# Position-bias tables read back from DRAM in final orientation, instead of turned on TensorE

## The chip, the cores and the metric

One Trainium2 chip, one core of it. The metric is the device time of one execution in microseconds (us). Engines: PE is TensorE, DVE is VectorE, ACT is ScalarE, POOL is GpSimd, SP is SyncE, which here only issues DMAs. Everything is fp32; the big products are split into a high and a low part and done as three products.

## The reference, cut to what matters

Two blocks of two layers each over 256 tokens of width 1024. The change touches only the position bias of the two attentions of the second block:

```python
REL_BUCKETS, REL_MAX_EXACT, REL_MAX_DIST, ATTN_HEADS = 32, 16, 128, 8

def t5_bucket(dist):                 # dist = query_pos - key_pos
    n = jnp.maximum(dist, 0)
    nf = jnp.maximum(n, 1).astype(jnp.float32)
    large = 16 + (jnp.log(nf / 16) / math.log(8) * 16).astype(jnp.int32)
    return jnp.where(n < 16, n, jnp.minimum(large, 31))
```

The logit of query q and key k in head h gets `rel_bias[t5_bucket(q - k), h]` added before the softmax. Keys after the query are masked; the window attention ("even" layer) also masks keys 128 or more behind. So the bias of a head depends on q - k alone: 384 numbers for each of 8 heads and 2 attentions hold all of it, and a 128 x 256 tile of logits needs them as 128 rows, each shifted by one against the row before it.

## The kernel before, in words

The activations lie feature by feature in SBUF (128 partitions, 256 tokens to the right). The weights stream from DRAM as 261 chunks of 128 x 1024 fp32 (512 KB). A chunk goes through four steps, one engine each:

1. SP issues its load into a ring of four buffers `raw` (`load_weights`, L423), once DVE is done with the chunk four before (`weight_lo`).
2. ACT copies it to `w_hi` (`convert`, L1146), once the load has landed and PE has finished the chunk four before.
3. DVE forms `w_lo` = raw - w_hi (L1576).
4. PE runs 24 matmuls on it, three for each of eight 128 x 128 tiles (`split_product`, L526 to L528).

SP's queue is one list in program order: weight chunks, chunks of the modulation weights (`ada`, 512 KB each, read by DVE in `modulate_loop`, L1591), and a few small loads. The stages follow one another on PE in the order of the table STAGES: attention of the first block, `ffn0_up`, `ffn0_down`, `gm_u0`, `gm_v`, `gm_u1`, `gm_out`, `ffn1_up`, `ffn1_down`, then the even layer (`even_s`, ...) and the odd layer (`odd_g`, `odd_k`, `odd_v`, `odd_q`, `odd_out`). Four of these stages (gm_u0, ffn1_up, even_s, odd_g) begin alike: their first weight chunk, the sums of squares of a norm (`sum_squares`), then a part of `turn_biases`, then the other chunks. PSUM results wait in four banks for DVE (`evacuate`), which needs the norm's reciprocal first.

The biases are made like this. At the start of ffn0_up, PE forms a table over the 384 distances for each head (`rel_table`), from a one-hot matrix and `rel_bias`; ACT copies it to `table` (8 partitions, 2 x 384). SP stores it in the DRAM tensor `bias_by_distance` (16 rows of 384, 24 KB), waits for the store (`table_stored`), and reads it back into `bias` (128 partitions x 16 heads x 256) with one skewed load: partition p starts p elements later in each row. DRAM addresses can only grow with the partition here, so the rows come out upside down. Each `turn_biases` part therefore multiplies two 128 x 512 slices with the anti-diagonal matrix `anti` (L824, two slices in each of the four parts), and ACT copies them back from PSUM with a scale (`bias_part`, L1358). PE waits on `bias_ready` in a few places afterwards. DVE adds `bias` to the logits in `beat_logits` (L1969), first in stage even_a, some 540 us after the table is made.

Around the skewed load SP's list reads: weight chunks 30 to 37, wait for the table, store, wait, skewed load, and then from the loop on: ada chunk 28, weight chunk 38, weight chunk 39, and so on.

Of the kernel before, what the change touches and what calls it, by code (L numbers as in the profile page):

```python
# [22 lines left out]
P = 128  # L23
D = 1024
KT = D // P
S = 256
# [14 lines left out]
ADA_MODS = 10  # L41

# [103 lines left out]
def build_program(nc, vecs, consts, gm_rows, c_rows, rel_ext, x_in, ctx_in, ada, weights,  # L146
# [10 lines left out]
    scratch = nc.dram_tensor("bias_by_distance", (16, MASKW), fp32, kind="Internal").ap()  # L157

    hold = ExitStack()
    with hold:  # L160
# [68 lines left out]
        anti = sb("anti", [P, P], fp32, late)  # L229
# [148 lines left out]
        class Attention:  # L378


            def __init__(self, name):
# [7 lines left out]
        table_sums, table_out, table_stored, table_skewed, bias_turned, bias_ready = (  # L389
            sem(n) for n in ("table_sums", "table_out", "table_stored", "table_skewed",  # L390
                             "bias_turned", "bias_ready"))
# [23 lines left out]
        def _(sp):  # L415
# [65 lines left out]
            sp.dma_start(anti[:], consts["anti"]).then_inc(table_in, 16)  # L481
# [38 lines left out]
        def _(pe):  # L520
# [291 lines left out]
            def rel_table():  # L812
                pe.wait_ge(table_in, 48)
# [12 lines left out]

            def ffn(up, down_, split, norm, then_turn):
# [4 lines left out]
                then_turn()  # L832
# [22 lines left out]
            turn_biases(0)  # L855
# [12 lines left out]
            pe.wait_ge(bias_ready, 2)  # L868
# [16 lines left out]
            ffn("ffn1_up", "ffn1_down", "ffn1", 3, lambda: turn_biases(1))  # L885
# [85 lines left out]
            def raw_start(name, stage_in, number, part):  # L971
# [3 lines left out]
                turn_biases(part)  # L975
# [4 lines left out]
            raw_start("even_s", "even_in", 4, 2)  # L980
# [6 lines left out]
            for g in range(5):  # L987
                late("even_a", act, [g])
                if g == 0:
                    pe.wait_ge(bias_ready, 6)  # L990
# [102 lines left out]
            raw_start("odd_g", "odd_in", 5, 3)  # L1093
# [5 lines left out]
            pe.wait_ge(bias_ready, 8)  # L1099
# [37 lines left out]
        def _(act):  # L1137
# [229 lines left out]
            def ffn(stage, norm_number, shift, g_, after_norm):  # L1367
                up, down_ = stage + "_up", stage + "_down"
                norm(norm_number)
                after_norm()  # L1370
# [41 lines left out]
            bias_part(0)  # L1412
# [36 lines left out]
            ffn("ffn1", 3, None, vec_column("norm_gain_2"), lambda: bias_part(1))  # L1449
# [3 lines left out]
            bias_part(2)  # L1453
# [70 lines left out]
            bias_part(3)  # L1524
# [35 lines left out]
        def _(dve):  # L1560
# [399 lines left out]
            norm(4, by_token=True)  # L1960
            def beat_logits(a, logits_, sinks, scale, bias_of, b):
# [405 lines left out]
```

## Time and profile before

| | |
|---|---|
| times of three executions | 990.61, 991.26 and 1313.31 us; median 991.26 |
| span of the profiled execution, first to last instruction | 987.1 us |
| PE busy / DVE busy / ACT busy / POOL busy | 943.5 / 706.0 / 538.3 / 309.0 us |
| DMA | 195.60 MB, 198 GB/s over the span |

The profiled execution has a span, and no time of its own that stands with the three; its span lies 3.5 to 4.2 us under the two times that agree. "Busy" counts the time an engine works on an instruction. The profile has several views: the page with its sums, a timeline of the instructions of one engine (with the idle time before an instruction and what ended it, in square brackets), sums by stretch with the granted TensorE clock (1.00 is full speed) and the DMA rate, the list of waits, and the chain of work that ended last, followed back from the last instruction.

### The profile page before, as it was taken

What the parts mean: (1) busy time and instruction counts of PE and PEld (TensorE: products, weight loads), DVE (VectorE), ACT (ScalarE), POOL (GpSimd) and SP (SyncE); (2) the same over time, 40 slices, a digit from 0 to 9 for tenths busy, and PEclk for the clock granted to TensorE, in tenths of its full rate; (3) what the DMA queues carried; (4) which work ended last, traced back from release to release, by engine and by line L of the source; (5) the groups of instructions that cost most, each with busy time, mean ns of one, the idle gap of its engine ahead of it and who ended that gap; (6) DMA issues with size and microseconds to landing.
All of it is one profiled execution on the core that took longest, in us unless ns stands there. A gap on an engine that the chain in (4) does not pass through costs nothing.

```text
span 987.1 us, 19548 instructions
## 1 busy us (share of the span) xinstructions
PE 943.5 (96%) x6882; PEld 871.3 (88%) x6882; DVE 706.0 (72%) x1132; ACT 538.3 (55%) x921; POOL 309.0 (31%) x272
## 2 busy tenths in 40 slices
PE   5988989999999999999979999999999999999996
PEld 5877556799999999988969999999999879899996
DVE  4997778678988777897886688555555773475664
ACT  3464655565765444654634666654444761674645
POOL 1942122237997111120051288640110000330012
PEclk9898999999999999999979999999999998999999
DMA  9856175168878777788615676555555332255521
GB/s 351 292 182 239 42 226 171 47 218 309 309 271 275 284 267 279 244 324 283 225 61 171 234 256 214 186 176 190 171 192 182 130 95 98 86 172 173 169 87 43
DMA packets 57052, 195.60 MB, mean 198 GB/s; under 512 B 6303, under 2 KB 9791, under 8 KB 56736
## 3 DMA queue, kind: packets, MB, share of 16 engines
q1 hardware_dynamic: 55312, 192.36, 56.7%
q0 software_dynamic: 1680, 2.44, 1.1%
q8 instruction: 37, 0.61, 0.2%
q14 instruction: 23, 0.19, 0.1%
HBM read 192.65 MB, written 1.07 MB: 196 GB/s over the span
## 4 chain that ended last, share of the span: by engine, by line
PE 85%; DVE 9%; ACT 2%; issue 2%; DMA 1%; POOL 0%; SPq 0%; DVEq 0%; ACTq 0%
PE bank L526 24%; PE bank L527 24%; PE bank L528 24%; DVE w_lo L1576 2%; PE bank L791 1%; PE bank L925 1%; PE bank L951 1%; PE bank L624 1%; PE bank L782 1%; DMA x<-x_in 1%; PE bank L824 1%; PE bank L633 1%; PE bank L879 1%; DVE ada_raw L1678 1%; DVE ada_raw L1591 1%
## 5 line engine op out<-in xcount | busy, mean ns | idle before, releaser
L1576 DVE TENSOR_TENSOR w_lo<-raw,w_hi 128x1024 fp32r<-128x1024 f32 (+1 forms) x261 | 340.0, 1304 | 108.0 <-ACT w_hi L1146 106.1
L1146 ACT ACTIVATE w_hi<-raw 128x1024 fp32r<-128x1024 f32 (+1 forms) x261 | 272.4, 1044 | 174.4 <-PE bank L528 166.4
L526 PE MATMUL bank<-act_hi,w_hi 128*128 128x258 f32 (+1 forms) x872 | 251.5, 288 | 0.0
L527 PE MATMUL bank<-act_lo,w_hi 128*128 128x258 f32 (+1 forms) x872 | 248.0, 284 | 0.0
L528 PE MATMUL bank<-act_hi,w_lo 128*128 128x258 f32 (+1 forms) x872 | 247.5, 284 | 0.0
L526 PEld LDWEIGHTS bank<-act_hi,w_hi 128*128 128x128 f32 x872 | 166.1, 190 | 3.3 <-issue 2.8
L527 PEld LDWEIGHTS bank<-act_lo,w_hi 128*128 128x128 f32 x872 | 166.1, 190 | 1.0 <-issue 1.0
L528 PEld LDWEIGHTS bank<-act_hi,w_lo 128*128 128x128 f32 x872 | 166.1, 190 | 0.0
L528 PE MATMUL bank<-hid_hi,w_lo 128*128 128x256 f32 x512 | 143.4, 280 | 0.0
L526 PE MATMUL bank<-hid_hi,w_hi 128*128 128x256 f32 x512 | 142.8, 279 | 0.0
L527 PE MATMUL bank<-hid_lo,w_hi 128*128 128x256 f32 x512 | 142.8, 279 | 0.0
L527 PEld LDWEIGHTS bank<-hid_lo,w_hi 128*128 128x128 f32 x512 | 96.3, 188 | 0.0
L528 PEld LDWEIGHTS bank<-hid_hi,w_lo 128*128 128x128 f32 x512 | 96.1, 188 | 0.0
L526 PEld LDWEIGHTS bank<-hid_hi,w_hi 128*128 128x128 f32 x512 | 95.7, 187 | 0.0
L2181 POOL TENSOR_TENSOR tile_f<-relu 128x256 f32<-128x256 f32 x64 | 83.3, 1301 | 31.5 <-ACT relu L1379 31.5
L2133 POOL TENSOR_TENSOR square_sum<-square_sum,sq 128x256 f32<-128x256 f32 x30 | 38.8, 1294 | 135.8 <-ACT sq L1178 135.8
L2185 POOL TENSOR_TENSOR hid_lo<-tile_f,hid_hi 128x256 f32 x64 | 72.6, 1134 | 18.0 <-POOL tile_f L2181 18.0
L1591 DVE CUSTOM_DVE_ANT_0 ada_raw<-ada_raw,silu_row 128x1024 f32<-128x1024 f32 x56 | 75.2, 1343 | 2.0 <-DMA ada_raw<-ada 1.8
L2125 POOL TENSOR_TENSOR s_lo<-tile_f,s_hi 128x256 fp32r<-128x256 f32 x24 | 23.1, 977 | 100.4 <-ACT s_hi L1151 100.4
L526 PE MATMUL bank<-s_hi,w_hi 128*128 128x256 f32 x192 | 53.9, 281 | 0.0
L527 PE MATMUL bank<-s_lo,w_hi 128*128 128x256 f32 x192 | 53.5, 279 | 0.0
L528 PE MATMUL bank<-s_hi,w_lo 128*128 128x256 f32 x192 | 53.4, 278 | 0.0
(349 smaller groups left out, 1812.7 us busy)
## 6 DMA issues: line engine op xcount, KB each, us to landing
raw<-weights SPq DMA_DIRECT2D x247, 512.0 KB, 3.6
ada_raw<-ada SPq DMA_DIRECT2D x88, 512.0 KB, 4.8
raw<-weights SPq DMA_DIRECT2D x14, 384.0 KB, 4.3
ada_more<-ada SPq DMA_DIRECT2D x8, 512.0 KB, 6.4
bias<-bias_by_distance SPq DMA_DIRECT2D x1, 2048.0 KB, 9.1
x<-x_in SPq DMA_DIRECT2D x1, 1024.0 KB, 7.3
ctx<-ctx_in SPq DMA_DIRECT2D x1, 1024.0 KB, 9.5
out<-result SPq DMA_DIRECT2D x4, 256.0 KB, 2.7
```

The source lines that it names most:

```text
L526: pe.matmul(dst, w[0], a[0], start=start, stop=False)
L527: pe.matmul(dst, w[0], a[1], start=False, stop=False)
L528: return pe.matmul(dst, w[1], a[0], start=False, stop=stop)
L624: last = pe.matmul(bank[at_bank][:, 0:S], mean[:], source[:, k, :], start=k == 0, stop=k == KT - 1)
L633: last = pe.matmul(bank[6 + k % 2][:, 0:2], first_ada(2 * k)[:, j * P:(j + 1) * P], silu_c[:, j, :], start=j == 0, stop=j == KT - 1)
L1146: act.activation(w_hi[:, slot, 0:width_of(c)], raw[:, slot, 0:width_of(c)], ACT.Copy).then_inc(weight_hi, 1)
L1576: dve.tensor_tensor(w_lo[:, slot, 0:w], raw[:, slot, 0:w], w_hi[:, slot, 0:w].bitcast(fp32), ALU.subtract).then_inc(weight_lo, 1)
L1591: dve.tensor_tensor_reduce(ada_raw[:, q, :], ada_raw[:, q, :], silu_row[:], 1.0, 0.0, ALU.mult, ALU.add, ada_col[:, q:q + 1]).then_inc(ada ...
L2125: pool.tensor_tensor(lo, tile_f32[:, i % 4, :], hi.bitcast(fp32), ALU.subtract).then_inc(split_lo, 1)
L2133: pool.tensor_tensor(square_sum[:], sq[:, 0, :] if k == 1 else square_sum[:], sq[:, k, :], ALU.add).then_inc(square_sums, 1)
L2181: pool.tensor_tensor(tile_f32[:, i % 4, :], relu[:, g % 2, :], relu[:, g % 2, :], ALU.mult).then_inc(hid_squared, 1)
L2185: pool.tensor_tensor(hid_lo[:, ds(it * 8 + g, 1), :], tile_f32[:, i % 4:i % 4 + 1, :], hid_hi[:, ds(it * 8 + g, 1), :].bitcast(fp32), ALU. ...
```

## The change

`bias_by_distance` becomes 16 copies of the table (384 KB), written by 16 stores one after the other on SP's queue. After all 16 have landed, eight loads read it back, each into 16 partitions of `bias`: within a load, partition p + j reads copy j and starts j elements earlier, so addresses grow with the partition and the rows come out the right way up. The scale moves into the copy of the table. `anti`, its load, the eight products and their eight copies go, and so do the waits on `bias_ready`; DVE waits once for all eight loads before the even layer.

```diff
+BIAS_COPIES = 16
-    scratch = nc.dram_tensor("bias_by_distance", (16, MASKW), fp32, kind="Internal").ap()
+    scratch = nc.dram_tensor("bias_by_distance", (BIAS_COPIES, 16, MASKW), fp32, kind="Internal").ap()
-        anti = sb("anti", [P, P], fp32, late)
...
-            sp.dma_start(anti[:], consts["anti"]).then_inc(table_in, 16)
...
             sp.wait_ge(table_out, 1)
-            sp.dma_start(scratch.rearrange("(t h) d -> h t d", t=2), table[:]).then_inc(table_stored, 16)
-            sp.wait_ge(table_stored, 16)
-            skewed = bass.AP(scratch.tensor, 0, [[1, P], [MASKW, 16], [1, S]])
-            sp.dma_start(bias[:], skewed).then_inc(table_skewed, 16)
+            for n in range(BIAS_COPIES):
+                sp.dma_start(scratch[n].rearrange("(t h) d -> h t d", t=2), table[:]).then_inc(table_stored, 16)
+            sp.wait_ge(table_stored, 16 * BIAS_COPIES)
+            for p in range(0, P, BIAS_COPIES):
+                skewed = bass.AP(scratch.tensor, P - 1 - p, [[16 * MASKW - 1, BIAS_COPIES], [MASKW, 16], [1, S]])
+                sp.dma_start(bias[p:p + BIAS_COPIES], skewed).then_inc(bias_in, 16)
...
-            def turn_biases(part):
-                if part == 0:
-                    pe.wait_ge(table_skewed, 16)
-                for i in (2 * part, 2 * part + 1):
-                    pe.matmul(bank[5 + i % 2][:], anti[:], bias[:, 2 * i:2 * i + 2, :],
-                              start=True, stop=True).then_inc(bias_turned, 1)
...
-            turn_biases(0)
...
-            pe.wait_ge(bias_ready, 2)
...
-            def bias_part(part):
-                for i in (2 * part, 2 * part + 1):
-                    act.wait_ge(bias_turned, i + 1)
-                    act.activation(bias[:, 2 * i:2 * i + 2, :],
-                                   bank[5 + i % 2][:].rearrange("p (a b) -> p a b", a=2),
-                                   ACT.Copy, scale=8.0 if i < 4 else math.sqrt(128.0)).then_inc(bias_ready, 1)
...
-                    last = act.activation(table[:, t, :], bank[5 + t][0:H, 0:MASKW], ACT.Copy)
+                    last = act.activation(table[:, t, :], bank[5 + t][0:H, 0:MASKW], ACT.Copy,
+                                          scale=8.0 if t == 0 else math.sqrt(128.0))
...
             norm(4, by_token=True)
+            dve.wait_ge(bias_in, 16 * P // BIAS_COPIES)
```

## Rows read from the trace of the kernel before

**Rows 1.** Page, first part: engine, busy us, share of the span, instructions.

```profile
PE 943.5 (96%) x6882; PEld 871.3 (88%) x6882; DVE 706.0 (72%) x1132; ACT 538.3 (55%) x921; POOL 309.0 (31%) x272
```

**Rows 2.** Page, the chain that ended last, shares by engine.

```profile
PE 85%; DVE 9%; ACT 2%; issue 2%; DMA 1%; POOL 0%; SPq 0%; DVEq 0%; ACTq 0%
```

**Rows 3.** Instructions of line L824: duration in ns (least, median, most), first and last start.

```profile
L824 PE MATMUL bank<-bias,anti x16: 592/592/676, 401.8 to 883.4; 128*128 128x512 f32 x16
```

**Rows 4.** The chain that ended last, in order of time: start, us, what.

```profile
401.93 1.72 PE bank L824 x4
...
749.50 1.82 PE bank L824 x4
```

**Rows 5.** Sums by stretch: us, then busy us (instructions) of each engine, clock, DMA.

```profile
398.00:424.00 26.00, 26.00 (x203) 24.94 (x202) 23.46 (x35) 16.82 (x26) 6.65 (x6) 1.00 0.70 231
```

**Rows 6.** Waits of ACT from 560 to 660 us: in total, times, longest.

```profile
ACT w_hi L1146 <- PE bank L528: 26.2, 31, 0.9
```

**Rows 7.** Timeline of ACT at the start of odd_g.

```profile
882.55 0.26 ACT L1365 ACTIVATE rstd_tok<-bank,eps 128x2 f32<-128x2 f32 x1
...
884.62 1.28 ACT L1527 ACT_TABLE_LOAD   x1
885.92 0.42 ACT L1527 ACTIVATE gate_o<-gate_o 128x256 f32<-128x256 f32 x1
886.24 1.04 ACT L1146 ACTIVATE w_hi<-raw 128x1024 fp32r<-128x1024 f32 x1
888.91 0.42 ACT L1527 ACTIVATE gate_o<-gate_o 128x256 f32<-128x256 f32 x1 [1.63 <-DVE gate_o L1635]
```

**Rows 8.** Timeline of DVE at the same place.

```profile
884.56 0.40 DVE L1635 TENSOR_TENSOR gate_o<-bank,rstd 128x256 f32<-128x256 f32 x1
```

**Rows 9.** Waits of PE from 870 us to the end.

```profile
PE bank L526 <- DVE ck_o L1635: 1.5, 1, 1.5
```

**Rows 10.** Timeline of SP: DMA issues in the earlier attention and in ffn0_up.

```profile
189.69 0.38 SPq L479 DMA_DIRECT2D onehot<-const_onehot  x1
190.11 0.30 SPq L480 DMA_DIRECT2D rel<-rel_ext  x1
...
229.63 0.34 SPq L489 DMA_DIRECT2D bias_by_distance<-table  x1
232.70 0.38 SPq L492 DMA_DIRECT2D bias<-bias_by_distance  x1
```

**Rows 11.** DMA issues: tensor, count, KB each, median us from issue to landing.

```profile
bias<-bias_by_distance SPq DMA_DIRECT2D x1, 2048.0 KB, 9.1
...
onehot<-const_onehot SPq DMA_DIRECT2D x1, 99.0 KB
```

**Rows 12.** Timeline of ACT in ffn0_up.

```profile
235.05 1.06 ACT L1146 ACTIVATE w_hi<-raw 128x1024 fp32r<-128x1024 f32 x1 [0.91 <-PE bank L528]
...
237.96 1.07 ACT L1146 ACTIVATE w_hi<-raw 128x1024 fp32r<-128x1024 f32 x1 [0.91 <-PE bank L528]
...
244.43 1.06 ACT L1146 ACTIVATE w_hi<-raw 128x1024 fp32r<-128x1024 f32 x1 [4.08 <-DMA raw<-weights]
```

**Rows 13.** Timeline of DVE in ffn0_up.

```profile
245.52 1.23 DVE L1576 TENSOR_TENSOR w_lo<-raw,w_hi 128x1024 fp32r<-128x1024 f32 x1 [1.22 <-ACT w_hi L1146]
```

**Rows 14.** Sums by stretch, as in rows 5; the last number is the DMA rate in GB/s.

```profile
190.60:191.40 0.80, 0.80 (x10) 0.80 (x9) 0.61 (x1) 0.09 (x1) 0.75 (x1) 1.00 0.47 128
...
233.70:240.00 6.30, 6.30 (x54) 6.30 (x54) 5.98 (x8) 3.94 (x7) 5.35 (x6) 1.00 1.04 352
242.00:249.00 7.00, 7.00 (x60) 7.00 (x59) 4.38 (x7) 4.31 (x7) 2.80 (x3) 1.00 1.03 408
```

**Rows 15.** Sums by stretch; the third number from the end is the granted clock.

```profile
91.60:98.40 6.80, 5.89 (x19) 5.08 (x19) 4.01 (x7) 0.20 (x1) 1.80 (x2) 0.50 0.88 339
...
126.00:129.20 3.20, 1.88 (x8) 0.97 (x7) 3.20 (x7) 2.58 (x5) 0.42 (x1) 0.99 0.91 165
129.20:132.60 3.40, 3.40 (x9) 2.62 (x10) 0.99 (x1) 1.16 (x3) 0.00 (x0) 0.50 0.98 367
```

More of the change, by code:

```diff
@@ L387, in build_program @@
         latent, window, blocks = Attention("latent"), Attention("window"), Attention("blocks")
-        table_sums, table_out, table_stored, table_skewed, bias_turned, bias_ready = (
-            sem(n) for n in ("table_sums", "table_out", "table_stored", "table_skewed",
-                             "bias_turned", "bias_ready"))
+        table_sums, table_out, table_stored, bias_in = (
+            sem(n) for n in ("table_sums", "table_out", "table_stored", "bias_in"))
         ln_counted, ln_var, ln_std, v_normed, ws_sums, ws_sum_ready, mixed = (
@@ L812, in rel_table @@
             def rel_table():
-                pe.wait_ge(table_in, 48)
+                pe.wait_ge(table_in, 32)
                 for t in range(2):
@@ L816, in rel_table, with ffn @@
                               start=True, stop=True).then_inc(table_sums, 1)
-            def turn_biases(part):
-                if part == 0:
-                    pe.wait_ge(table_skewed, 16)
-                for i in (2 * part, 2 * part + 1):
-                    pe.matmul(bank[5 + i % 2][:], anti[:], bias[:, 2 * i:2 * i + 2, :],
-                              start=True, stop=True).then_inc(bias_turned, 1)
-            def ffn(up, down_, split, norm, then_turn):
+            def ffn(up, down_, split, norm, then=None):
                 hidden = split0[split + "_hid"]
@@ L831, in ffn @@
                 sum_squares(norm)
-                then_turn()
+                if then is not None:
+                    then()
                 run(stage)
@@ L884, in _ @@
                             it=it, per=4, a_wait=lambda k: split0["gm_s"] + k + 1))
-            ffn("ffn1_up", "ffn1_down", "ffn1", 3, lambda: turn_biases(1))
+            ffn("ffn1_up", "ffn1_down", "ffn1", 3)
             def scores(att_, heads, u):
@@ L969, in window_heads, with raw_start @@
                 return bq[r, h // 2, :], bk[r, :], lambda kt: bv_tok[:, kt, (h % 2) * 64:(h % 2 + 1) * 64]
-            def raw_start(name, stage_in, number, part):
+            def raw_start(name, stage_in, number):
                 wait = {"a_wait": lambda k: RAW[stage_in] + k + 1, "a_sem": raw_lo}
@@ L974, in raw_start @@
                 sum_squares(number, by_token=True)
-                turn_biases(part)
             def window_beat(b):
                 beat(window, window_heads, b, prob, prob_t, pair, True, split0["even_o"])
-            raw_start("even_s", "even_in", 4, 2)
+            raw_start("even_s", "even_in", 4)
             late("even_s", act, range(1, 4))
@@ L989, in _ @@
                 if g == 0:
-                    pe.wait_ge(bias_ready, 6)
                     pe.wait_ge(v_tok, 1)
@@ L1091, in odd_o_wait @@
                 return split0["odd_o"] + k + 1
-            raw_start("odd_g", "odd_in", 5, 3)
+            raw_start("odd_g", "odd_in", 5)
             late("odd_g", act, range(1, 8))
@@ L1098, in _ @@
                            groups=(bank_free[n], bank_free[n + 1]))
-            pe.wait_ge(bias_ready, 8)
             for g in range(8):
@@ L1365, in norm, with ffn @@
                     act.activation(rstd_tok[:, 0:2], bank[4][:, S:S + 2], ACT.Sqrt, bias=eps[:]).then_inc(std_tok, 1)
-            def ffn(stage, norm_number, shift, g_, after_norm):
+            def ffn(stage, norm_number, shift, g_, after_norm=None):
                 up, down_ = stage + "_up", stage + "_down"
                 norm(norm_number)
-                after_norm()
+                if after_norm is not None:
+                    after_norm()
                 with act.Fori(0, 4) as it:
@@ L1447, in _ @@
                         square_residual("gm_out", j // 2, it, 4)
[L1449 removed]
+            ffn("ffn1", 3, None, vec_column("norm_gain_2"))
             norm(4, by_token=True)
[L1453 removed]
             for g in range(6):
@@ L2251, in constants @@
     masks[:, 2 * S:] = (s_ // 64 == c_ // 64) & (s_ <= c_)
-    return {"const": const, "rope": rope, "onehot": onehot, "anti": np.eye(P, dtype=np.float32)[::-1].copy(),
+    return {"const": const, "rope": rope, "onehot": onehot,
             "masks": masks}
```

2 lines of the change are left out of this document (removed).

## The prediction

> **What bounds the kernel now.** I read the page first. PE is busy for 943.5 us of the span [rows 1], and the chain that ended last runs on PE for 85% of it [rows 2]. So an instruction that leaves PE's list is worth its own time there, as long as the next thing that PE needs is ready; and anything that makes a weight chunk late is paid in full. Then I read three places: the products with `anti` in the chain, the first chunks of the four stages that hold them, and SP's queue around the skewed load in ffn0_up. In that last place the reader is to see that PE itself does not stop, but that its supply is close to running dry: ACT waits 4.08 us for a weight chunk there [rows 12].
>
> **The products and their PSUM copies go.** The trace lists 16 matmul records at L824, two for each product [rows 3]. They are pipelined, so their median of 592 ns is not what each holds PE for; the chain gives that: 1.72 us for a part of two products. Four parts stand in the chain: 1.72 us in gm_u0, 1.72 in ffn1_up, 1.82 in even_s and 1.82 in odd_g (the two lengths that occur are shown) [rows 4]. Together 7.1 us. Is PE's next need ready in each?
> - gm_u0: PE is busy for all 26 us of the stage [rows 5]. DVE is close behind with 23.46 us, but with four PSUM banks and four weight buffers between the two, PE can run 1.7 us closer to it without meeting it. DVE carries the chain for a while at the end of gm_u1, but that stretch starts with a conversion which PE's progress releases, so it moves as a whole. Gain 1.7.
> - ffn1_up: ACT's conversions wait for PE, 31 times in 100 us [rows 6]: the supply is paced by PE, not the other way round. Gain 1.7.
> - even_s: the same pattern, conversions that wait for PE. Gain 1.8.
> - odd_g: here not all arrives. ACT and DVE pass work back and forth: DVE evacuates a gate, ACT applies SiLU, then converts a chunk, DVE makes w_lo, and only then evacuates the next gate. A turn takes 888.91 - 885.92 = 2.99 us [rows 7], a little longer than a chunk on PE. PE meets the end of that loop when it waits 1.5 us for `ck_o` [rows 9]. What counts is when the loop starts. ACT is free after 882.55 + 0.26 = 882.8; without the two copies the table load of 1.28 us ends at 884.1, and the first SiLU is held by DVE's evacuation, which ends at 884.96 [rows 7, 8]. It starts near 885.0 instead of 885.92. Gain 0.9 and not 1.8, and the wait for `ck_o` grows from 1.5 to 2.4 us.
>
> Sum of the gains: 1.7 + 1.7 + 1.8 + 0.9 = 6.2 us after rounding. The other six bias copies of ACT lie beside PE's work and are worth nothing alone, the waits on `bias_ready` and the load of `anti` likewise. The scale on the table copy costs nothing: the copy is there anyway. DVE's new wait for the eight loads has all of DVE's work from the even layer on behind it, but the loads are issued 500 us earlier.
>
> **SP's queue grows.** 16 stores and 8 loads take the place of one store and one load, ahead of ada 28 and weight chunk 38. Two short issues on SP follow one another in 190.11 - 189.69 = 0.42 us [rows 10]. The last store is therefore issued 15 x 0.42 = 6.3 us after the first, and with the same time from issue to the end of the wait (232.70 - 229.63 = 3.07 us [rows 10]) the first skewed load goes out at 239.0 instead of 232.7. The issues of the other seven loads (under 0.4 us each) hide behind the transfer of the first ones.
>
> **The eight loads themselves.** They move the same 2048 KB (2.10 MB) as the one load did, but each reaches 16 partitions and not 128. No row shows that. Two bounds and a near row:
> - At the rate of the old load, 352 GB/s [rows 14], the transfer takes 6.0 us. A gain against this has no reason: the same bytes in the same 1 KB pieces.
> - If the rate went with the partitions reached, it would be 16/128 of the weights' 408 GB/s [rows 14], that is 51 GB/s, and 41 us.
> - The nearest row is the one-hot table: 99 KB onto 33 partitions [rows 11]. It moved in a stretch that ran at 128 GB/s [rows 14], a third of the other rates. At 128 GB/s the eight loads take 16.4 us. I take this value. It is too kind because 16 partitions are fewer than 33, and too harsh because so short a transfer contains its own start.
>
> The Trainium skill, page "SBUF — State Buffer", section "Door 1: The DMA port swizzle", says that the rate depends on how many of 16 ports the partitions reach, and that partitions 0 to 15 reach four; it gives 104 GB/s measured at 1 MiB. By it the loads would take an estimated 20.2 us, and the sum would come out at 1005.4. No run here shows it yet.
>
> **What the delay costs on PE.** Before, the bias landed at 232.70 + 9.1 = 241.8 [rows 10, 11]; ada 28 and chunk 38 came after it, and ACT could convert chunk 38 at 244.43, 2.6 us later [rows 12]; DVE was done with it at 246.75 [rows 13]. When does PE need it? A conversion of chunk c + 4 waits for PE to end chunk c. The one at 237.96, of chunk 37, was released by PE's end of chunk 33, near 237.9, and PE takes 237.96 - 235.05 = 2.91 us for a chunk [rows 12]. It ends chunk 37 at 237.9 + 4 x 2.9 = 249.5. So the slack was 2.8 us. Now the bias lands at 241.8 + 6.3 + (16.4 - 6.0) = 258.5, ACT starts on chunk 38 at 261.1, DVE is done at 263.4, and PE has stood still for 13.9 us. After that it should not stop again: the following chunks come at full DMA rate, 1.3 us each at 408 GB/s, and ACT and DVE need less time for one than PE does. The delay is paid once and nothing gives it back, since the whole rest hangs on PE.
>
> **The clock.** A pause brings a second price. Where PE was busy for 1.88 of 3.2 us, the next 3.4 us were granted 0.50, the lower level of 1.2 GHz; another such stretch lasted 6.8 us [rows 15]. Half of the work time in it is lost: 1.7 to 3.4 us. I take 2.6. Such stretches lie at other places too, around 500 and 835 us, and shifting the work against them can change the time by 2 us either way; the sum leaves that at zero.
>
> **The sum.** Against the profiled span: 987.1 - 6.2 + 13.9 + 2.6 = 997.4 us. The span lies 4.2 us under the median of the runs, 991.26, so the time is 1001.6 us, about 1% slower than before.
>
> **Rivals.**
> 1. *The rate belongs to the DMA engines, not to the partitions: not slower.* The transfer takes 6.0 us again. The 16 stores alone then make chunk 38 late by 6.3 us, against a slack of 2.8: PE stops for 3.5 us. With 1.7 us of low clock: 991.26 - 6.2 + 3.5 + 1.7 = 990.3; without it 988.6. For it: 16 rows can still occupy 16 DMA engines, and all packets are of the old size. Against it: the one-hot row. It holds for a transfer of up to some 7 us; from there on the change loses.
> 2. *A quarter of the full rate.* 408 / 4 = 102 GB/s gives 20.6 us and a pause of 13.9 + 4.2 = 18.1 us: 1005.8. For it: 16 partitions are half of the 33 that ran at 128 GB/s. The Trainium skill's rule of four ports, in the section named above, is this case.
> 3. *The rate goes with the partitions reached.* 41 us, a pause of 38.5 us: 1026, slower by over 2%. Values above 26 us of transfer already pass that line (1011.1). Against it: by the same scaling the one-hot load should have had 105 GB/s, and it had 128 with its start included.
> 4. *The stores hold the queue longer.* If each of the 16 also cost DMA time that the next must wait for, up to the 3.07 us that one took alone, the delay would be 46 us. Only the first part of this is plausible: 24 KB move in well under an issue time at any rate seen. I count it within case 3.
> 5. *The change doesn't do what it says.* If the gains in the four stages were covered by DVE and not real, 6.2 us would be missing: 1007.8.
>
> **How the numbers follow.** Chances: forecast (transfer 12 to 18.5 us) 0.38; rival 1 0.17; rival 2 (up to 24 us) 0.30; rivals 3 and 4 0.10; rival 5 0.05. The forecast's own range: a transfer of 12 us with 1.7 us of clock gives 996.3, one of 18.5 us with 3.4 gives 1004.5. For 8 times in 10 the range needs the forecast, rival 2 with its upper end at 1010, and most of rival 1: 988 to 1010. A difference of 2% is 19.8 us, about what a measurement of this kernel can tell from no change. Faster by 2% would need more than all gains together: 0.01. Slower by 2% is rivals 3 and 4: 0.11. Within: 0.88.
>
> **What would show it.** In the profile after: no L824 and no L1358; SP's timeline with 16 stores 0.4 us apart and the first load of `bias` near 239; a DMA rate between 239 and 256 near 128 GB/s, where it is 352 before; ACT waiting some 20 us for `raw` and PE waiting some 14 us for `w_lo` near 250, followed by a few us at clock 0.50; from gm_u0 on, each of the four stages shorter by 1.7 to 1.8 us except odd_g; the wait for `ck_o` at 2.4 us. The prediction is wrong if the eight loads run at another rate: each microsecond of transfer is a microsecond of time, once the slack of 2.8 us is gone.

## The result, and the profile after

The changed kernel takes 1001.50 us (median of 4 runs, 1000.39 to 1006.17) against 990.93 for the kernel before on the same chip: ratio 1.012, 95% interval 1.010 to 1.014. It is about 1% slower. One of the four runs of the kernel before took 1313.31 us, is a slow one, and doesn't count in the ratio. The profiled execution took 1000.39 us with a span of 998.6. The page's first part and the chain's shares, beside [rows 1, 2]:

```profile
PE 940.2 (94%) x6866; PEld 871.0 (87%) x6866; DVE 706.0 (71%) x1132; ACT 532.8 (53%) x913; POOL 311.3 (31%) x272
...
PE 77%; DVE 11%; ACT 3%; issue 3%; DMA 3%; SPq 1%; POOL 0%; DVEq 0%; ACTq 0%
```

PE has its 16 matmul records less, and 3.3 us less of busy time. But the chain now runs on PE for 77% of the span instead of 85%, and SP's queue is in it with 1%. The chain, in order of time, says where (start, us, what):

```profile
233.07 1.12 SPq L488
236.89 2.62 DMA bias_by_distance<-table
244.34 17.47 DMA raw<-weights
261.92 1.07 ACT w_hi L1134
263.01 1.24 DVE w_lo L1556
```

The end of the execution is traced back to a weight chunk that was issued at 244.34 and took 17.47 us to land, and from there to the sixteen stores. Nothing is wrong with that chunk: it stands behind the eight loads. SP's timeline (start, us, issues), beside [rows 10]:

```profile
230.20 7.14 SPq L488 DMA_DIRECT2D bias_by_distance<-table  x16
239.53 3.79 SPq L492 DMA_DIRECT2D bias<-bias_by_distance  x8
...
244.34 0.97 SPq L422 DMA_DIRECT2D raw<-weights  x2
```

The sums by stretch show what the transfers did (length, busy us of PE, PEld, DVE, ACT and POOL, clock, DMA share, GB/s), beside [rows 14, 15]:

```profile
234.00:239.00 5.00, 5.00 (x43) 5.00 (x43) 4.68 (x6) 2.94 (x6) 4.47 (x5) 1.00 0.46 52
242.00:257.00 15.00, 8.10 (x67) 7.89 (x66) 0.00 (x0) 0.00 (x0) 0.59 (x1) 0.86 1.16 117
260.00:268.00 8.00, 3.63 (x17) 3.64 (x18) 5.90 (x9) 5.66 (x10) 4.28 (x3) 0.50 1.03 410
```

The stores run at 52 GB/s, the eight loads at 117 (2.10 MB, so 17.9 us), the weight chunks after them at 410 again. The busy share of the DMA engines is above 1 during the slow loads: a busy engine is not a fast one. On ACT and PE it looks like this (timeline of ACT; then two of PE's waits: in total, times, longest):

```profile
261.92 1.06 ACT L1134 ACTIVATE w_hi<-raw 128x1024 fp32r<-128x1024 f32 x1 [21.02 <-DMA raw<-weights]
```

```profile
PE bank L526 <- DVE w_lo L1556: 15.7, 2, 14.3
...
PE bank L526 <- DVE ck_o L1615: 2.4, 1, 2.4
```

ACT waits 21.02 us for the chunk where it waited 4.08 [rows 12], and PE stands still for 14.3 us near 250. The other times of that row (1.4 us) and the wait for `ck_o` (1.5 us before [rows 9]) lie in the odd layer. From 270 to 400 us PE is busy all the time, at full clock:

```profile
270.00:400.00 130.00, 130.00 (x1094) 1.00 0.80 280
```

Where between the beginning and the end does the time come and go? The matmul at L610 begins a norm in five places, so its starts cut the span into pieces. Before:

```profile
214.98 0.59 PE L610 MATMUL bank<-square_sum,mean 128*128 128x256 f32 x2
400.90 0.59 PE L610 MATMUL bank<-square_sum,mean 128*128 128x256 f32 x2
561.56 0.59 PE L610 MATMUL bank<-square_sum,mean 128*128 128x256 f32 x2
747.70 0.59 PE L610 MATMUL bank<-square_sum,mean 128*128 128x256 f32 x2
880.33 0.59 PE L610 MATMUL bank<-square_sum,mean 128*128 128x256 f32 x2
```

After:

```profile
215.53 0.59 PE L610 MATMUL bank<-square_sum,mean 128*128 128x256 f32 x2
418.35 0.59 PE L610 MATMUL bank<-square_sum,mean 128*128 128x256 f32 x2
574.26 0.59 PE L610 MATMUL bank<-square_sum,mean 128*128 128x256 f32 x2
758.67 0.59 PE L610 MATMUL bank<-square_sum,mean 128*128 128x256 f32 x2
891.15 0.59 PE L610 MATMUL bank<-square_sum,mean 128*128 128x256 f32 x2
```

The pieces changed by +0.55 (start), +16.90 (ffn0), -4.75 (gm), -1.73 (ffn1), -0.15 (even layer) and +0.68 us (odd layer, to the end of the span): +11.5 in all. ffn1's piece is the textbook one: 1.72 us of products gone [rows 4], 1.73 us won. The others hold products and clock together. Stretches at the lower clock (clock third from the end), after:

```profile
252.70:269.70 17.00, 5.33 (x25) 0.50 1.07 301
...
512.10:522.30 10.20, 8.15 (x32) 0.50 0.20 69
839.80:850.00 10.20, 10.20 (x42) 0.50 0.11 45
921.70:925.10 3.40, 3.40 (x18) 0.50 0.80 270
```

and before:

```profile
497.80:511.50 13.70, 10.56 (x42) 0.50 0.11 39
832.30:839.10 6.80, 6.80 (x31) 0.50 0.00 0
```

Half of PE's busy time in such a stretch is lost. In ffn0 that is 2.7 us, and 14.3 + 2.7 = 17.0 is the piece. In the even layer the stretch at 1.2 GHz is 3.4 us longer than before and costs 1.7 us more, so the 1.8 us of products arrive as 0.15. In the odd layer a new stretch of 3.4 us stands right behind the wait for `ck_o` and costs 1.7 us; with the 0.9 us won that makes the +0.7 seen. In gm the stretch lost 10.56 / 2 = 5.3 us before and 8.15 / 2 = 4.1 after; with 1.7 us of products that gives 2.9 of the 4.75 us. The other 1.8 us of that piece are not explained, and they are not the change's alone. Each profile is one execution, and the same piece (155.91 us long here) took 155.9 us in e1 and e11 too, but 157.6 to 157.7 in e3, e4, e6, e7 and e8, which have no products either and whose low stretch there is also 10.2 us long.

### The profile page after: what moved, and what is told of

It reads as the page before. It is cut to its first block, busy times and chain, and to the rows that moved or that the text cites. A ratio compares the mean times of both kernels' runs of the same rounds, so it can differ in the third digit from the quotient of the medians.

```text
span 998.6 us, 19529 instructions
## 1 busy us (share of the span) xinstructions
PE 940.2 (94%) x6866; PEld 871.0 (87%) x6866; DVE 706.0 (71%) x1132; ACT 532.8 (53%) x913; POOL 311.3 (31%) x272
## 4 chain that ended last, share of the span: by engine, by line
PE 77%; DVE 11%; ACT 3%; issue 3%; DMA 3%; SPq 1%; POOL 0%; DVEq 0%; ACTq 0%
PE bank L526 22%; PE bank L528 22%; PE bank L527 22%; DVE w_lo L1556 3%; DMA raw<-weights 2%; ACT w_hi L1134 1%; PE bank L791 1%; DVE products L1658 1%; PE bank L916 1%; PE bank L942 1%; PE bank L624 1%; DVE ada_raw L1658 1%; PE bank L782 1%; DMA x<-x_in 1%; SPq L488 1%
## 5 line engine op out<-in xcount | busy, mean ns | idle before, releaser
L526 PE MATMUL bank<-act_hi,w_hi 128*128 128x258 f32 (+1 forms) x872 | 251.7, 289 | 14.3 <-DVE w_lo L1556 14.3
L526 PEld LDWEIGHTS bank<-act_hi,w_hi 128*128 128x128 f32 x872 | 167.4, 192 | 16.8 <-issue 16.4
L2162 POOL TENSOR_TENSOR tile_f<-relu 128x256 f32<-128x256 f32 x64 | 86.5, 1352 | 45.1 <-ACT relu L1361 45.1
## 6 DMA issues: line engine op xcount, KB each, us to landing
bias<-bias_by_distance SPq DMA_DIRECT2D x8, 256.0 KB, 10.6
```

Of the source, the lines that this page charges most:

```text
L526: pe.matmul(dst, w[0], a[0], start=start, stop=False)
L2162: pool.tensor_tensor(tile_f32[:, i % 4, :], relu[:, g % 2, :], relu[:, g % 2, :], ALU.mult).then_inc(hid_squared, 1)
```

## The experiments

All times are medians; a ratio is to the kernel before, on the same chip, with its 95% interval. It is 990.45 us for the first four kernels, 991.23 for e5 to e8, 992.14 for e9 and e10, 991.18 for e11 and e12.

### Taking the change apart: e1 to e4

**e1_products_gone_only.** The removal alone, with one store and one load as before.

```diff
-            for n in range(BIAS_COPIES):
-                sp.dma_start(scratch[n].rearrange("(t h) d -> h t d", t=2), table[:]).then_inc(table_stored, 16)
-            sp.wait_ge(table_stored, 16 * BIAS_COPIES)
-            for p in range(0, P, BIAS_COPIES):
-                skewed = bass.AP(scratch.tensor, P - 1 - p, [[16 * MASKW - 1, BIAS_COPIES], [MASKW, 16], [1, S]])
-                sp.dma_start(bias[p:p + BIAS_COPIES], skewed).then_inc(bias_in, 16)
+            sp.dma_start(scratch[0].rearrange("(t h) d -> h t d", t=2), table[:]).then_inc(table_stored, 16)
+            sp.wait_ge(table_stored, 16)
+            skewed = bass.AP(scratch.tensor, 0, [[1, P], [MASKW, 16], [1, S]])
+            sp.dma_start(bias[:], skewed).then_inc(bias_in, 16)
```

> The changed kernel with the DMAs of before: one store, one skewed load of 128 partitions. Left out: the turning, so the bias rows stand upside down. It measures the gain alone. My theory (the four parts are worth 1.7, 1.7, 1.8 and 0.9 us): 991 - 6.2 = 984.7 us, give or take 1.7 us for a stretch of low clock more or less; PE does not stop near 250 us. Rival (the gains are covered by DVE and ACT): 990 to 991.

Measured: 984.62 us, ratio 0.994 (0.992 to 0.997). The removal is worth 5.8 us (3.4 to 7.7 by the interval), where the sum had 6.2. Its profile loses and gains in the same places as the changed kernel's from gm on: -4.75 (gm), -1.69 (ffn1), -0.22 (even layer), +0.70 us (odd layer), and 0.00 in ffn0. PE's waits show `ck_o` at 2.4 us, as forecast:

```profile
PE bank L524 <- DVE ck_o L1613: 2.4, 1, 2.4
```

**e2_sixteen_stores_one_load.** The sixteen stores as changed, the one load of e1.

> The changed kernel with its 16 stores, but one skewed load of 128 partitions as before. Left out: the turning. It measures the stores. The load starts 6.3 us late as in the changed kernel; of that 2.8 us are slack, so PE stops for 3.5 us and loses about 1.7 us more to low clock: 984.7 + 5.2 = 990 us. Rival (the delay comes from the loads alone, the stores are hidden): 985.

Measured: 990.58 us, ratio 1.000 (0.997 to 1.002). PE waits 2.4 us for `w_lo` near 254. The load runs at 360 GB/s, the stores at 52:

```profile
238.00:243.00 5.00, 5.00 (x44) 5.00 (x43) 4.68 (x6) 2.94 (x6) 4.47 (x5) 1.00 0.45 52
245.00:250.00 5.00, 5.00 (x43) 5.00 (x42) 0.72 (x2) 0.09 (x1) 1.51 (x2) 1.00 1.06 360
```

The stores alone eat up what the products were worth: 6.0 us more than e1 by the medians, which scatter (986.95 to 995.08 us here, 982.05 to 989.85 in e1). The profile holds 2.4 us of pause with no low clock behind it, and ffn0 is 3.3 us longer than in e1. Another 2.4 us lie in gm, where the stretch at half clock is 13.7 us long instead of 10.2; whether the stores cause that is not shown. Its execution also lost some 3 us to a stretch at half clock near 145 us, before anything that the edit touches. This kernel is what rival 1 supposed (990.3 us, with a pause of 3.5).

**e3_one_store_eight_loads.** One store, and eight loads of 16 neighbouring partitions, all from the same copy.

```diff
-                skewed = bass.AP(scratch.tensor, P - 1 - p, [[16 * MASKW - 1, BIAS_COPIES], [MASKW, 16], [1, S]])
+                skewed = bass.AP(scratch.tensor, p, [[1, BIAS_COPIES], [MASKW, 16], [1, S]])
```

> The changed kernel with one store, and eight loads of 16 neighbouring partitions each, all from the one copy. Left out: the turning. It measures the loads. Theory (a load that reaches 16 neighbouring partitions runs at a third of the rate, near 118 GB/s as in the changed kernel): 17.8 us of transfer in place of 6.0, a stop of 17.8 - 6.0 - 2.8 = 9.0 us, 2.6 us of low clock: 996 us, and near 118 GB/s in the stretch. Rival (what slows the loads is that every partition reads another copy, 24 KB apart in DRAM): with one copy the rate is 350 GB/s again and the time 985.

Measured: 995.95 us, ratio 1.006 (1.004 to 1.008), a pause of 9.0 us:

```profile
236.00:252.00 16.00, 13.94 (x116) 13.73 (x114) 5.07 (x7) 3.32 (x6) 5.30 (x5) 1.00 1.17 114
```

One copy or sixteen, the loads run at the same rate. So the distance between the copies in DRAM doesn't set it. What is left is the split into eight loads of 256 KB and the partitions that each reaches; e4 and e11 keep the split and change the partitions.

**e4_loads_every_eighth_partition.** The changed kernel; each load reaches partitions i, i + 8, i + 16, ...

```diff
-            for p in range(0, P, BIAS_COPIES):
-                skewed = bass.AP(scratch.tensor, P - 1 - p, [[16 * MASKW - 1, BIAS_COPIES], [MASKW, 16], [1, S]])
-                sp.dma_start(bias[p:p + BIAS_COPIES], skewed).then_inc(bias_in, 16)
+            for i in range(P // BIAS_COPIES):
+                skewed = bass.AP(scratch.tensor, P - 1 - i, [[16 * MASKW - 8, BIAS_COPIES], [MASKW, 16], [1, S]])
+                sp.dma_start(bias[i:P:8], skewed).then_inc(bias_in, 16)
```

> The changed kernel in full (16 stores, right result), only that load i fills partitions i, i + 8, i + 16 and so on instead of 16 neighbours. Theory A (the rate depends on which partitions a load reaches; the Trainium skill, page SBUF - State Buffer, section Door 1, has 16 ports, of which 16 neighbours reach four and every eighth partition reaches eight): twice the rate, near 236 GB/s, 8.9 us of transfer, a stop of 5.4 us, time 992. Theory B (the rate depends on how many partitions a load reaches): 118 GB/s and 1001.5 us, as the changed kernel.

Measured: 994.74 us, ratio 1.004 (1.002 to 1.006). The pause is 7.2 us and the rate 218 GB/s:

```profile
246.00:255.00 9.00, 8.24 (x69) 8.04 (x67) 0.00 (x0) 0.00 (x0) 0.74 (x1) 1.00 1.13 218
```

Still sixteen partitions and the same bytes to a load, at nearly twice the rate. The count of partitions is not what sets it. The time lies between the two expectations but nearer to that of the ports; 2.10 MB at this rate are 9.6 us, where the rate of the changed kernel gives 17.9.

### Which partitions, and which of the stores' costs: e11, e12, e5

**e11_loads_every_second_partition.** The same with sixteen partitions two apart, within 31.

```diff
+            for p in (32 * u + i for u in range(4) for i in range(2)):
+                skewed = bass.AP(scratch.tensor, P - 1 - p, [[16 * MASKW - 2, BIAS_COPIES], [MASKW, 16], [1, S]])
+                sp.dma_start(bias[p:p + 31:2], skewed).then_inc(bias_in, 16)
```

> The changed kernel with its sixteen stores; each of the eight loads reaches sixteen partitions two apart (0, 2, ..., 30, then 1, 3, ..., 31, and so on) instead of sixteen neighbours. The whole result is computed. Rows so far: 117 GB/s for sixteen neighbours, 218 for sixteen that are eight apart. Theory A (paths into SBUF are shared by blocks of four neighbouring partitions, and eight such blocks below partition 64 have a path each): the load touches eight blocks, as many paths as in e4, so 218 GB/s, pause 7 to 9 us, 994 to 996 us. Theory B (what counts is how far the partitions spread over SBUF): 31 partitions wide is nearer to the neighbours than to e4's 121, so 120 to 150 GB/s, pause 11 to 14 us, 999 to 1001.5 us. The Trainium skill, page SBUF — State Buffer, section Door 1: The DMA port swizzle, is theory A: by its table these sixteen reach eight of 16 ports, with 218 GB/s as the upper limit.

**e12_one_store_four_loads_every_fourth.**

```diff
+            for i in range(4):
+                skewed = bass.AP(scratch.tensor, i, [[4, 32], [MASKW, 16], [1, S]])
+                sp.dma_start(bias[i:P:4], skewed).then_inc(bias_in, 16)
```

> One copy of the table and one store, as in e3, but four loads of 32 partitions each, four apart (0, 4, ..., 124 and so on), in place of eight of 16 neighbours. The rows of the bias come upside down, so this kernel leaves out the turning of the bias. Theory A of e11 (blocks of four have the path): 32 partitions touch all 32 blocks, so the load runs at the full rate of 350 to 410 GB/s, the pause is under 1 us and the time that of e1, 984 to 986 us. Theory B' (the rate grows with the partitions reached in one load, and 128 are needed for the full rate): 218 to 250 GB/s, 8.5 to 9.6 us of transfer, a pause of 1 to 2 us, 986 to 989 us. The Trainium skill, page SBUF — State Buffer, last part on two DMAs, says that only one transfer over all 128 partitions reaches all 16 ports, while its table of ports gives all 16 to these 32 partitions; the window's rate decides between the two.

Measured: e11 994.16 us, ratio 1.004 (1.002 to 1.005), pause 7.6 us, 195 to 207 GB/s; e12 984.96 us, ratio 0.993 (0.992 to 0.995), no pause, 352 GB/s. Sums by stretch of e11, without PE:

```profile
242.00:250.00 8.00, 1.00 1.12 207
...
244.00:250.00 6.00, 1.00 1.15 195
```

and of e12:

```profile
236.00:241.00 5.00, 5.00 (x44) 5.00 (x43) 4.69 (x8) 3.47 (x6) 4.05 (x5) 1.00 1.06 352
```

Both bear out theory A, that what counts is which paths into SBUF a load reaches. Sixteen neighbours touch 4 blocks of four partitions and get 117 GB/s; sixteen that are two apart touch 8 blocks and get 195 to 207; 32 partitions four apart touch all 32 blocks and get what one load of 128 gets. A spread over 31 partitions does nearly as well as one over 121. A path of its own for each block does not fit all rows, though: the sixteen of e4, eight apart, touch 16 blocks and get 218 GB/s, about the rate of 8 blocks. Some blocks must share a path. The Trainium skill, page "SBUF — State Buffer", section "Door 1: The DMA port swizzle", has this as a table of 16 ports with 27.2 GB/s each: 4 ports (109), 8 ports (218), 16 ports. In it partitions 32 apart share a port, which gives the loads of e4 and of e11 8 ports both. The trace agrees with its order and, within 11%, with its figures for 4 and for 8 ports; for the stores' 8 partitions the table gives 2 ports, an estimated 54 GB/s, and the row shows 52, but no run here changes the partitions of the stores alone. Its 436 for all 16 is not reached by the skewed loads (352 to 360). The same page, in the section "Can I just issue two DMAs to hit both halves?", says that the only way to hit all 16 ports is one transfer that spans all 128 partitions. The loads of e12 stretch over nearly all of them but reach only 32 each, and they run at the full rate of this place; so here the spread was enough, without the count of 128.

**e5_table_on_128.** Are the stores slow because there are sixteen, or because they read 8 partitions? Here the table's matmul makes all sixteen copies, on 128 partitions, and two stores take them out; the loads are those of e4.

```diff
-            rel = sb("rel", [33, H], fp32, ffn)
+            rel = sb("rel", [33, P], fp32, ffn)
...
+            sixteen_times = bass.AP(rel_ext.tensor, 0, [[H, 33], [0, BIAS_COPIES], [1, H]])
+            sp.dma_start(rel[:].rearrange("r (n h) -> r n h", h=H), sixteen_times).then_inc(table_in, 16)
...
+            for t in range(2):
+                sp.dma_start(scratch[:, t * H:(t + 1) * H, :],
+                             table[:, t, :]).then_inc(table_stored, 16)
+            sp.wait_ge(table_stored, 32)
```

> The whole result is computed. The relative bias table is built sixteen times over by the matmul itself (its 8 columns repeated to 128), so it stands on 128 partitions; two stores of 192 KB from all 128 partitions replace sixteen of 24 KB from 8, and the eight loads reach every eighth partition, as in e4 (994.7 us). My theory (the stores are bound by the 8 partitions they read, 52 GB/s, and the loads by the partitions they write): the first load goes out 3 to 4 us after the first store, not 9.3; the loads land about 5.7 us earlier than in e4, the pause of TensorE before chunk 38 falls from 7.2 to 1 to 2 us, and the time to 986 to 989 us. If the stores are bound by their count or by the small runs of 1536 bytes, which stay the same: the first load again 9 us after the first store, pause 7 us, 994.5 us.

Measured: 990.75 us, ratio 1.000 (0.999 to 1.002). SP's timeline:

```profile
230.50 1.28 SPq L489 DMA_DIRECT2D bias_by_distance<-table  x2
234.53 5.78 SPq L494 DMA_DIRECT2D bias<-bias_by_distance  x8
```

The first load goes out 4.0 us after the first store and not 9.3, with the same bytes stored in the same 1536-byte runs. So the runs of 1536 bytes alone don't hold the stores back. But the edit changes two things, the partitions read (8 to 128) and the number of stores (16 to 2), and 14 issues fewer, at the median of 0.34 us below, are already 4.8 us of the 5.3 us saved. The traces say a little more. This is how long the issues of the stores took (ns: least, median, most), in the changed kernel and in e6 below, where each store stands alone:

```profile
L488 SPq DMA_DIRECT2D bias_by_distance<-table x16: 293/336/1116, 230.2 to 236.9; - x16
L494 SPq DMA_DIRECT2D bias_by_distance<-table x16: 339/340/347, 236.7 to 324.4; - x16
```

In the burst some issues are held up, and a DMA packet of 1536 bytes takes 222 ns (median of 256), against 65 ns in e5 and 65 in e6. The packets of a single store from 8 partitions are therefore not slow; those of sixteen in a row are. Whether they wait for the path of their 8 partitions or for something else that small stores share is not shown: sixteen small stores from other partitions would have to be tried.

The rest of my expectation was too low: the pause is 2.7 us, not 1 to 2, and the time misses the expected 986 to 989. The pause brings a stretch at half clock behind it, which I had left out:

```profile
250.00:253.40 3.40, 0.73 (x5) 0.53 (x4) 2.07 (x4) 2.64 (x4) 1.23 (x1) 0.92 1.03 410
253.40:256.00 2.60, 2.60 (x13) 2.60 (x13) 2.39 (x3) 2.44 (x5) 2.33 (x3) 0.50 1.03 410
```

Here a pause of 2.7 us had such a stretch behind it; e2's of 2.4 us had none. With its stores and loads as good as I could make them in one burst, the change only breaks even.

### Is it the rate, or the burst: e6, e7, e8, e9

**e6_spread_over_the_loop.** The stores and loads of the changed kernel, as slow as they are, but in other places of SP's list.

```diff
-            with sp.Fori(1, 12) as it:
+            for k in range(1, 9):
+                for j in range(8):
+                    if j % 2 == 0:
+                        load_ada(ADA_EARLY + j // 2 + 4 * k)
+                    load_weights(30 + j + 8 * k)
+                    if k < 5 and j % 2 == 1:
+                        n = 4 * (k - 1) + j // 2
+                        sp.dma_start(scratch[n].rearrange("(t h) d -> h t d", t=2), table[:]).then_inc(table_stored, 16)
+                    elif k >= 5 and j % 4 == 3:
+                        if k == 5 and j == 3:
+                            sp.wait_ge(table_stored, 16 * BIAS_COPIES)
+                        p = BIAS_COPIES * (2 * (k - 5) + j // 4)
+                        skewed = bass.AP(scratch.tensor, P - 1 - p, [[16 * MASKW - 1, BIAS_COPIES], [MASKW, 16], [1, S]])
+                        sp.dma_start(bias[p:p + BIAS_COPIES], skewed).then_inc(bias_in, 16)
+            with sp.Fori(9, 12) as it:
```

> The whole result is computed, with the changed kernel's sixteen stores and eight loads exactly as they are, at 117 GB/s; only their places in SyncE's list differ: four stores in each of the next four passes of the weight loop (one after every second weight chunk), two loads in each of the four passes after those (one after every fourth chunk). My theory (the loss is one run of 27 us of queue time put ahead of a ring that covers 2.8 us, while the queue has room between weight loads): each single load of 256 KB takes 2.2 us and is covered, no pause of TensorE over 1 us anywhere in ffn0, time 984.6 as with the products gone alone, 983 to 987 us. If the loss were in what the transfers take from the weight loads wherever they stand (27 us of a queue that is mostly busy): several pauses of 1 to 2 us in ffn0, 990 to 998 us.

Measured: 985.22 us, ratio 0.995 (0.993 to 0.996). The same 24 transfers cost 16.9 us in one place (1001.50 - 984.62) and nothing measurable in 24 places: e1, without them, has the ratio 0.994 too. PE has no wait that the trace lists between 225 and 440 us, with all the loads in between, and ffn0 takes 185.94 us where the kernel before takes 185.93. The loads are no faster for standing alone: the packets of each take 2.2 to 2.7 us from first to last; in the burst 2.4 to 2.7, after the first load. The first and the last of the eight:

```profile
335.75 0.43 SPq L500 DMA_DIRECT2D bias<-bias_by_distance  x1
...
417.03 0.43 SPq L500 DMA_DIRECT2D bias<-bias_by_distance  x1
```

This settles the main step of the loss: it was the burst, against a slack of 2.8 us, and not the bandwidth taken from the weights.

**e7 and e8: the odd layer.** In odd_g, ACT converts the next chunk before it waits for the gate; e7 adds this to e6, **e8_weights_first_in_odd_g_alone** to the changed kernel.

```diff
+                convert(chunk0["odd_g"] + g + 4)
                 act.wait_ge(evacuated, group0["odd_g"] + g + 1)
                 act.activation(gate_o[:, g, :], gate_o[:, g, :], ACT.Silu).then_inc(gated, 1)
-                convert(chunk0["odd_g"] + g + 4)
```

> e6, and in odd_g ScalarE converts the next weight chunk before it waits for the gate of its group, where the kernels before and after do the reverse. The whole result is computed. My theory (from the first gate on, ScalarE's wait for the VectorE evacuation makes each weight chunk late, 3.0 us a group against 2.7 us that TensorE needs, and the wait of 2.4 us for ck_o and the stretch of 3.4 us at half clock behind it are its end): the wait for ck_o goes, the clock stays up there, 2.4 + 1.7 = 4.1 us less than e6, 980 to 981 us. If the groups run at 3.0 us for another reason (VectorE's own order, the loads): no more than 0.5 us less than e6.

> The changed kernel with the one swap of e7 in odd_g and nothing else. The whole result is computed. My theory: as in e7, 4.1 us less than the changed kernel's 1001.5, so 997 to 998 us, with the pause of 14.3 us in ffn0 unchanged. If the swap only helps where the rest has moved (a stretch at half clock falls elsewhere): the gain differs from that of e7 by the 1.7 us of a stretch, or is zero.

Measured: e7 982.75 us, ratio 0.993 (0.991 to 0.995), 2.5 us under e6; e8 999.95 us, ratio 1.009 (1.007 to 1.012), 1.6 us under the changed kernel, with overlapping intervals. Two rows of ACT in odd_g of e7, to be read beside [rows 7]:

```profile
886.81 1.06 ACT L1142 ACTIVATE w_hi<-raw 128x1024 fp32r<-128x1024 f32 x1 [1.52 <-PE bank L536]
...
889.70 1.06 ACT L1142 ACTIVATE w_hi<-raw 128x1024 fp32r<-128x1024 f32 x1 [1.52 <-PE bank L536]
```

A turn takes 889.70 - 886.81 = 2.89 us and is released by PE; before it took 2.99 and was released by DVE. The wait for `ck_o` falls to 0.6 us:

```profile
PE bank L534 <- DVE ck_o L1623: 0.6, 1, 0.6
```

So the loop between DVE and ACT, on which the forecast put 0.9 us, is there and the swap opens it. My expectation of 4.1 us was too high: it counted 1.7 us of clock, but in e6 no low stretch stood behind that wait, although the wait was 2.4 us there too. And 0.6 us of the wait remain. In e8 the wait is 0.6 us as well, and the new stretch near 921 is gone:

```profile
842.90:849.70 6.80, 6.80 (x30) 0.50 0.01 2
866.80:870.20 3.40, 3.40 (x18) 0.50 0.51 159
915.00:930.00 15.00, 14.39 (x122) 1.00 0.54 176
```

The two low stretches of its even layer are together as long as the single one of the changed kernel (10.2 us), so they cost nothing more. From the last norm on, e8's profile is 2.7 us shorter than the changed kernel's. But its gm piece is 1.7 us longer (157.61 against 155.91), with a low stretch of the same 10.2 us, and so only 1.1 us is left between the two executions. The edit does not touch gm. A difference of 1.7 us in one execution can thus come from somewhere else, and e8's 1.6 us by the medians, with four runs, don't settle whether the swap is worth 1.8 or 3.5 us.

**e9_two_stores_fast_loads_spread.** e5's two stores and e4's loads, spread, and the swap of e7: the best kernel of this study.

> The whole result is computed. The table on 128 partitions with its two stores (e5), the loads to every eighth partition (e4) two to a pass of the weight loop (e6), and weights first in odd_g (e7). My theory (transfers that lie between weight loads are covered, so their rate no longer matters): 982 to 983.5 us, the same as e7 with its sixteen stores and loads at 117 GB/s. If the slow loads of e7 still cost the weight loads something: 1 to 3 us less than e7.

Measured: 981.38 us, ratio 0.991 (0.987 to 0.995). Against e7 with its slow transfers 1.4 us less, with overlapping intervals: once spread, the rate matters little or not at all. I can't tell 0 from 2 us here.

### Gain and loss together: e10

**e10_transfers_changed_products_kept.** The kernel before, with only the stores and loads changed:

```diff
-            sp.dma_start(scratch.rearrange("(t h) d -> h t d", t=2), table[:]).then_inc(table_stored, 16)
-            sp.wait_ge(table_stored, 16)
-            skewed = bass.AP(scratch.tensor, 0, [[1, P], [MASKW, 16], [1, S]])
-            sp.dma_start(bias[:], skewed).then_inc(table_skewed, 16)
+            for n in range(BIAS_COPIES):
+                sp.dma_start(scratch[n].rearrange("(t h) d -> h t d", t=2), table[:]).then_inc(table_stored, 16)
+            sp.wait_ge(table_stored, 16 * BIAS_COPIES)
+            for p in range(0, P, BIAS_COPIES):
+                skewed = bass.AP(scratch.tensor, p, [[16 * MASKW + 1, BIAS_COPIES], [MASKW, 16], [1, S]])
+                sp.dma_start(bias[p:p + BIAS_COPIES], skewed).then_inc(table_skewed, 16)
```

> The kernel before with its anti-diagonal products and their copies kept; only the one store and one load are replaced by the changed kernel's sixteen stores and eight loads of 16 partitions, with the skew turned so that rows land upside down as the products need them. The whole result is computed. My theory (gain and loss are independent: the products are worth 5.8 to 6.6 us, the transfers cost 16.5 to 17): 1007 to 1008 us, a pause of about 14.3 us before chunk 38 as in the changed kernel. If part of the gain only exists because the pause moved what follows it (the stretches at half clock), or the reverse: 1003 to 1005 us, or 1010 and more.

Measured: 1009.25 us, ratio 1.018 (1.015 to 1.022), a pause of 14.0 us:

```profile
PE bank L529 <- DVE w_lo L1579: 15.4, 2, 14.0
```

The transfers cost 17.1 us here, the products gave 5.8 in e1, and 17.1 - 5.8 = 11.3 stands beside the 10.6 us of the whole change. Gain and loss are independent, within what these runs can tell.

## Why the prediction was right, step by step

The forecast was 1001.6 us and 1001.5 was measured. The path was the right one: the products give a few us, the transfers delay chunk 38 past a slack of 2.8 us, and PE stands still for the rest. That the two numbers agree to 0.1 us is luck: the forecast span was 997.4 us and the profiled one 998.6, and terms of the sum were off in both directions.

- **The products, 6.2 us.** e1: 5.8. The sum held and its terms did not: gm gave 4.75 us for 1.7, the even layer 0.15 for 1.8, the odd layer lost 0.7 where 0.9 was to be won, and only ffn1 gave what it should, 1.73 for 1.72. In the even and the odd layer the clock took back what the products gave; that gm gave more than its products made up for it, and this is luck. Rival 5 (gains not real) is out by e1's interval.
- **odd_g, 0.9 instead of 1.8.** The forecast that `ck_o` would be waited for 2.4 us instead of 1.5 came out to the digit, in the changed kernel and in e1, and e7 opened the loop that causes it.
- **Stores, first load 6.3 us later.** The first load follows the first store by 239.53 - 230.20 = 9.3 us; the forecast had 9.4. The number held and its reason held in part: I took it as fifteen issue times of 0.42 us. The issues take 7.14 us, 0.45 each, but their median is 0.34 and some are held up (1.12 the longest), while the stores run at 52 GB/s, where 16 x 24 KB (0.39 MB) need 7.6 us. The two times are nearly the same here. I had dismissed rival 4 because 24 KB move in well under an issue time "at any rate seen"; at 52 GB/s they take 0.47 us, just over one. With two stores from 128 partitions (e5) the first load goes out after 4.0 us; how much of that is the issues and how much the transfer, e5 does not separate.
- **Transfer, 16.4 us at 128 GB/s.** 117 GB/s and 17.9 us. The one-hot row, with 33 partitions in a stretch that held its own start and end, was near by luck: e3, e4, e11 and e12 show that the rate goes with which partitions a load reaches, and 33 neighbours touch more blocks of four than 16 do. The mechanism was that of rival 2, at a rate between its 102 and my 128. The Trainium skill's estimate of 20.2 us was too long, since its 104 GB/s is for one transfer of 1 MiB, and here eight in a row ran at 117; its rule for the cause was the right one.
- **The pause, 13.9 us.** 14.3. ACT got chunk 38 at 261.92 where 261.1 was forecast. Of the 1.5 us more of transfer 0.8 arrived there. The forecast had also put the old transfer at 6.0 us; in the trace the packets of the old load run from 233.73 to 241.25, 7.5 us, and those of the eight from 240.44 to 258.03, 17.6 us. The transfer grew by 10.1 us, where the forecast had 16.4 - 6.0 = 10.4: both transfers were taken too short, and that cancels.
- **The clock, 2.6 us.** 2.7 in ffn0. Elsewhere the stretches came out differently, as the forecast had allowed: 1.2 us less lost in gm, 1.7 more in the even layer, 1.7 more in the odd layer. e1 has the same three, without a pause in ffn0, so they are not the pause's doing.
- **Paid once, nothing gives it back.** The changed kernel shows no other pause before gm_u0: PE is busy for 130.00 of 130.00 us from 270 to 400. e10 shows that the loss is the same with the products kept, and e6 that without the burst ffn0 is as long as before.

## What to carry to other kernels

Before a transfer is put ahead of a ring of weight loads, work out how long the ring can do without: here 2.8 us. What is longer should be cut into pieces and spread over the loop; 24 slow transfers that cost 17 us in one burst cost nothing measurable in 24 gaps. And choose the partitions of a small DMA by the paths that they reach: sixteen that are two or eight apart are served at nearly twice the rate of sixteen neighbours. Don't count on a row of small stores being bound by its issues alone: sixteen from 8 partitions ran at 52 GB/s.

## What the runs showed of the hardware

- DMA rate by the partitions that one transfer reaches: 16 neighbours 114 to 117 GB/s; 16 two apart 195 to 207; 16 eight apart 218; 32 four apart 352; all 128 348 to 360 for the same skewed source.
- Sixteen stores of 24 KB in a row from 8 neighbouring partitions: 52 GB/s, 222 ns for a packet of 1536 bytes; one such store alone: 65 ns for a packet. What they share in the burst is not shown.
- The clock falls during a long pause and comes back late: in the 17.0 us at 1.2 GHz around the pause of 14.3 us, PE was busy for 5.33 us, and half of these are the price.
- Nine of the kernels without the products wait 2.3 to 2.4 us for `ck_o`. Six of them (the changed kernel, e1, e2, e4, e5, e11) have 3.4 us at half clock behind it, and three (e3, e6, e12) have none. What decides between the two I did not settle.
